# Streaming expert weights: a seventh weight buffer, and a token gather that reads the unscaled residual

## The reference

```python
h = rms_norm_2(x, norm_ffn_g[layer])          # x * rsqrt(mean(x*x) + eps) * gain
x = x + hier_moe(h, ...)                      # top-1 group of 4, then top-2 of its 8 experts

# hier_moe, for each chosen (token, expert):
#   y = gate * ((silu(h @ w_gate[e]) * (h @ w_up[e])) @ w_down[e])
```

## Time and profile before

| | |
|---|---|
| median of the runs | 1615.85 us |
| profiled execution, first to last instruction | 1614.8 us |
| TensorE busy | 1349.9 us (84%) |
| VectorE busy | 381.9 us (24%) |
| mean DMA rate over the span | 308 GB/s |
| DMA rate within the expert layers | 428 GB/s |

### The profile page before, as it was taken

How to read it: one execution, slowest core, us unless ns; L and a number is a source line. 1 busy time by engine, 2 the same in 40 slices (tenths; PEclk the granted TensorE clock), 3 DMA queues, 4 the chain that set the end, 5 groups by cost and what they waited for, 6 DMA issues and landing times. The chain is left out here.

```text
span 1614.8 us, 22089 instructions
## 1 busy us (share of the span) xinstructions
PE 1349.9 (84%) x9414; PEld 723.8 (45%) x9414; DVE 381.9 (24%) x787; ACT 278.1 (17%) x545; POOL 96.3 (6%) x98
## 2 busy tenths in 40 slices
PE   7999999999999999676676677899998667667676
PEld 3755457544879664232232232556553223232232
DVE  2331333313375531010010000257421001000011
ACT  1122310313223121210000000105211101111010
POOL 0000000000000006294000000000000000000000
PEclk9999999999999999989899898999999988899889
DMA  9822443234521199999999999934689999999997
GB/s 385 268 110 104 156 181 132 79 125 173 215 105 56 42 426 422 429 428 429 429 429 429 428 429 428 403 120 169 264 345 422 429 429 428 428 428 429 429 429 328
DMA packets 42092, 497.05 MB, mean 308 GB/s; under 512 B 6448, under 2 KB 9264, under 8 KB 11568
## 3 DMA queue, kind: packets, MB, share of 16 engines
q1 hardware_dynamic: 42032, 496.17, 74.5%
HBM read 494.06 MB, written 2.10 MB: 307 GB/s over the span
## 5 line engine op out<-in xcount | busy, mean ns | idle before, releaser
L2657 PE MATMUL banks<-weight_ring,arena 128*32 128x512 f32 x1920 | 286.2, 728 | 183.7 <-DMA weight_ring<-in_moe_weights 183.2
L2657 PEld LDWEIGHTS banks<-weight_ring,arena 128*32 128x32 f32 x1920 | 60.0, 121 | 389.2 <-DMA weight_ring<-in_moe_weights 201.0
L2580 DVE TENSOR_TENSOR arena<-arena,banks 64x512 f32<-64x512 f32 x32 | 22.1, 690 | 695.0 <-ACT arena L2528 694.0
L808 PE MATMUL banks<-weight_ring,hT 128*128 128x512 f32 x384 | 170.1, 600 | 1.3 <-DMA weight_ring<-in_ring_weights 1.3
L2668 PE MATMUL banks<-weight_ring,arena 128*32 128x512 f32 x1016 | 120.4, 602 | 27.6 <-issue 14.7
L2639 PE MATMUL banks<-arena,x_normed 128*128 128x64 f32 x1024 | 120.0, 276 | 0.0
L2639 PEld LDWEIGHTS banks<-arena,x_normed 128*128 128x128 f32 x1024 | 119.5, 195 | 0.0
L808 PEld LDWEIGHTS banks<-weight_ring,hT 128*128 128x128 f32 x384 | 73.0, 193 | 88.1 <-issue 86.3
L322 PE MATMUL banks<-weight_ring,hT 128*128 128x512 f32 x256 | 112.3, 593 | 0.0
L2528 ACT ACTIVATE arena<-banks 64x512 f32<-64x512 f32 x32 | 18.9, 591 | 522.1 <-PE banks L2657 522.1
L2698 PE MATMUL banks<-arena 64*128 64x512 f32 x240 | 59.6, 615 | 21.0 <-ACT arena L2534 21.0
(11 more groups left out here) (489 smaller groups left out, 1373.3 us busy)
## 6 DMA issues: line engine op xcount, KB each, us to landing
weight_ring<-in_moe_weights SPq DMA_DIRECT2D x183, 2048.0 KB, 26.2
weight_ring<-in_ring_weights SPq DMA_DIRECT2D x36, 2048.0 KB, 8.4
arena<-in_moe_weights SPq DMA_DIRECT2D x4, 2048.0 KB, 10.0
weight_ring<-in_ring_weights SPq DMA_DIRECT2D x4, 1024.0 KB, 4.8
mix<-in_moe_weights SPq DMA_DIRECT2D x2, 2048.0 KB, 16.4
arena<-in_moe_weights SPq DMA_DIRECT2D x3, 1024.0 KB, 13.1
hT<-in_moe_weights SPq DMA_DIRECT2D x2, 1024.0 KB, 9.9
arena<-in_c_even SPq DMA_DIRECT2D x1, 1440.0 KB, 6.4
```

What stands on the lines that cost most here:

```text
L808: ins = pe.matmul(bank, g.hT[:, k, half * P:(half + 1) * P], w[:, k, :], start=(k == 0), stop=(k == KT - 1))
L2580: dve.tensor_tensor(hid[0:2 * CAP, :], sil[0:2 * CAP, :], b_gu[2 * CAP:4 * CAP, :], ALU.mult).then_inc(s_h, 1)
L2657: ins = pe.matmul(b_gu[q:q + CAP, :], xg[:, 2 * quarter + k, e * CAP:(e + 1) * CAP], up_w(where, quarter, e)[:, which, k, :], start=(quart ...
```

## The change

- One more buffer of a full chunk, `g.spare`, holds (1,4). The room for it comes from the scratch that the compiler object reserves (`dynamic_dma_scratch_size=512`).
- `x_normed` is no longer filled by the router (`scale_x` is gone, and the squares go to a scratch that lies in `xg`), so a half of (1,5) goes there. The gather multiplies `g.x` itself, and the row factor 1/rms is multiplied into the selection matrix: `pick` now makes `Pm` (0/1) and, behind a wait, `Pr` = `Pm` times `rstd`.
- (1,5)'s other half goes into ring slot 0 in ly = 0, and into `xT_flat` in ly = 1.
- In ly = 0, (2,0) to (2,4) are issued when quarters 1, 2, 3 and the down halves of pair 0 are done, and (2,5) after pair 1's second down half. In ly = 1, (2,0) to (2,5) are issued after the six parts of pair 0.

```diff
+        self.spare = sb("spare_weights", [P, SW])[:, :]
+        self.xs_flat = self.xs[:, :, :].rearrange("p a d -> p (a d)")
...
@@ first expert layer, SyncE
             weights(1, 0, extra[0][0], second)
             weights(1, 1, extra[1][0], second)
+            weights(1, 4, g.spare, second)
+            sp.dma_start(g.xs_flat, A["moe_weights"][0, 1, 5][:, 0:2048]).then_inc(second[5], 16)
             router.fourth(sp)
...
@@ second expert layer, SyncE
+            weights(1, 4, g.spare, second)
             sp.wait_ge(s_prj, 5)
             weights(0, 0, ring[0], first)
...
             weights(1, 0, extra[0][0], second)
+            sp.dma_start(g.xs_flat, A["moe_weights"][1, 1, 5][:, 2048:SW]).then_inc(second[5], 16)
             sp.wait_ge(s_on, TT)
...
-            sp.dma_start(router.xT_flat, A["moe_weights"][1, 1, 4][:, 0:2048]).then_inc(second[4], 16)
+            sp.dma_start(router.xT_flat, A["moe_weights"][1, 1, 5][:, 0:2048]).then_inc(second[5], 16)
...
@@ VectorE
-        self.scale_x(dve, 1)
...
-        def pick(i):
-            dve.tensor_tensor(Pm, slots, of_pair(rankm, i), ALU.is_equal).then_inc(s_pm, 1)
+        def pick(i, n):
+            dve.tensor_tensor(Pm, slots, of_pair(rankm, i), ALU.is_equal).then_inc(s_eq, 1)
+            dve.wait_ge(s_eq, n + 1)
+            dve.tensor_tensor(Pr, Pm.rearrange("p a e j -> p a (e j)"),
+                              router.rstd.unsqueeze(2).to_broadcast([P, TT, 2 * CAP]), ALU.mult).then_inc(s_pm, 1)
...
@@ SyncE, expert phase
-        for j in range(4, 6):
-            released(j - 4, 0, 1)
-            load(1, 1, j)
+        if ly == 0:
+            released(0, 0, 1)
+            sp.dma_start(sixth[1], A["moe_weights"][ly, 1, 5][:, 2048:SW]).then_inc(landed[1][5], 16)
         for j in range(SLOTS):
-            released((2, 3, 4, 5, 4, 5)[j], 0, 1 if j < 4 else 2)
-            load(2, 2, j)
+            if j + turned < SLOTS:
+                released(j + turned, 0, 1)
+            else:
+                released(5, 0, 2)
+            load(2, j)
...
@@ TensorE, gather
-  g.xs[:, tt, k * P:(k + 1) * P], Pm[:, tt].rearrange("p e j -> p (e j)")
+  g.x[:, tt, k * P:(k + 1) * P], Pr[:, tt, :]
```

More of the change, by code:

```diff
@@ L45 @@
 MOE_AT = ODD_PAR
-MOE_SIZE = 3080
+MOE_SIZE = 3208
 SPLIT_AT = MOE_AT + MOE_SIZE
@@ L49 @@
 LAST_AT = EXTRA_AT + 2 * SW
-ARENA = 16960
-TURNED = 2
+ARENA = 17088
+TURNED = 1
 IN_ORDER = (4, 5, 0, 1, 2, 6, 3, 7)
@@ L336, with __init__ @@
 class TileNorm:
-    def __init__(self, g, sems, k, at, gain, banks):
+    def __init__(self, g, sems, bases, at, gain, banks):
         self.g, self.gain, self.banks = g, gain, banks
@@ L343, in __init__, with after @@
         self.s_sq, self.s_eps, self.s_rt, self.s_xs, self.s_tr, self.s_hT = \
-            (Counted(sem, k * n) for sem, n in zip(sems, (4, 2, 2, 2, 4, 4)))
+            (Counted(sem, base) for sem, base in zip(sems, bases))
+    def after(k):
+        return tuple(k * n for n in (4, 2, 2, 2, 4, 4))
     def sems(g, name):
@@ L472, in first_layers @@
     norm_sems = TileNorm.sems(g, "first_norm")
-    n_in = [TileNorm(g, norm_sems, 2 * l, (128, 144, 192)[l], gcol[l], (2, 3)) for l in range(DEPTH + 1)]
-    n_ple = [TileNorm(g, norm_sems, 2 * l + 1, 160 + 16 * l, None, (2, 3)) for l in range(DEPTH)]
+    n_in = [TileNorm(g, norm_sems, TileNorm.after(2 * l), (128, 144, 192)[l], gcol[l], (2, 3)) for l in range(DEPTH + 1)]
+    n_ple = [TileNorm(g, norm_sems, TileNorm.after(2 * l + 1), 160 + 16 * l, None, (2, 3)) for l in range(DEPTH)]
     layer = FirstSems.layers(g)
@@ L1369, in _ @@
                     router.inverse(dve, 0)
-                    router.scale_x(dve, 0)
                 if j == 2:
@@ L2245, in __init__ @@
         self.Pm = g.take(TT * 2 * CAP).rearrange("p (a e j) -> p a e j", a=TT, e=2)
+        self.Pr = g.take(TT * 2 * CAP).rearrange("p (a j) -> p a j", a=TT)
         self.w1 = self.Pm.rearrange("p a e j -> p a (e j)")[:, :, 0:NE]
@@ L2248, in __init__ @@
         self.PT = g.take(S)
-        self.xg = g.take(KT * 2 * CAP).rearrange("p (k j) -> p k j", k=KT)
+        xg = g.take(KT * 2 * CAP)
+        self.squared = xg[:, 0:HALF]
+        self.xg = xg.rearrange("p (k j) -> p k j", k=KT)
         self.hidT = g.take(4 * 2 * CAP).rearrange("p (f j) -> p f j", f=4)
@@ L2273, in squares @@
         act.wait_ge(self.s_x, j + 1)
-        act.activation(self.g.xs[:, tt, half], self.g.x[:, tt, half], ACT.Square,
+        act.activation(self.squared, self.g.x[:, tt, half], ACT.Square,
                        accum_out=self.part[:, j:j + 1]).then_inc(self.s_sq, 1)
@@ L2438, in expert_functions @@
     gcol, sil, hid, gate, rankm = router.gcol, router.sil, router.hid, router.gate, router.rankm
-    Pm, Pg, PT, xg, hidT, y = router.Pm, router.Pg, router.PT, router.xg, router.hidT, router.y
+    Pm, Pr, Pg, PT, xg, hidT, y = router.Pm, router.Pr, router.Pg, router.PT, router.xg, router.hidT, router.y
     s_pm, s_P, s_Pt, s_PTc = router.s_pm, router.s_P, router.s_Pt, router.s_PTc
@@ L2444, in expert_functions @@
     landed = g.moe_landed[ly]
-    fifth = [ring[0]] if ly == 0 else [router.xT_flat, ring[0][:, 0:2048]]
-    at_pair = ([[w] for w in ring], extra + [fifth, [ring[1]]], [[ring[(j + 2) % SLOTS]] for j in range(SLOTS)])
+    sixth = [g.xs_flat, ring[0][:, 0:2048]] if ly == 0 else [router.xT_flat, g.xs_flat]
+    turned = 1 - ly
+    at_pair = ([[w] for w in ring], extra + [[g.spare], sixth], [[ring[(j + turned) % SLOTS]] for j in range(SLOTS)])
     def up_w(where, j, e):
@@ L2462, in expert_functions @@
     s_da, s_dn, s_yc = (g.sem(n_ + k) for k in ("down_half", "down", "y_copied"))
-    s_sub, s_add = g.sem(n_ + "ranks_lowered"), g.sem(n_ + "added")
+    s_sub, s_add, s_eq = g.sem(n_ + "ranks_lowered"), g.sem(n_ + "added"), g.sem(n_ + "P_compared")
     s_sum = [g.sem(n_ + f"summed_{b}") for b in range(4)]
@@ L2482, in released, with load @@
             sp.wait_ge(*((s_gu, n * 4 + (more * 4 + j - 3)) if j < 4 else ((s_da, s_dn)[j - 4], n + more)))
[L2485 to L2491, removed]
-        for j in range(4, 6):
-            released(j - 4, 0, 1)
-            load(1, 1, j)
-        for j in range(SLOTS):
-            released((2, 3, 4, 5, 4, 5)[j], 0, 1 if j < 4 else 2)
-            load(2, 2, j)
+        def load(pair, j):
+            sp.dma_start(at_pair[2][j][0], A["moe_weights"][ly, pair, j]).then_inc(landed[2][j], 16)
+        if ly == 0:
+            released(0, 0, 1)
+            sp.dma_start(sixth[1], A["moe_weights"][ly, 1, 5][:, 2048:SW]).then_inc(landed[1][5], 16)
+        for j in range(SLOTS):
+            if j + turned < SLOTS:
[3 more added lines that the diff above has]
+            load(2, j)
         if ly == 0:
@@ L2506, in sync @@
                     released(j, t * NP + i, 3)
-                    load(2, i + 3, j)
+                    load(i + 3, j)
             with sp.If(t < T - 1):
@@ L2511, in sync @@
                         released(j, t * NP, pair + NP)
-                        load(2, pair, j)
+                        load(pair, j)
         g.limit = len(g.chunks)
@@ L2587, in advance @@
             gated(of_next, n + 1)
-        pick(0)
+        pick(0, 0)
         router.largest(dve)
@@ L2594, in vector @@
         gated(0, 0)
-        pick(1)
+        pick(1, 1)
         router.count_turns(dve)
@@ L2604, in vector @@
                 advance(t * NP + i, i + 1)
-                pick(i + 2)
+                pick(i + 2, t * NP + (i + 2))
             advance(t * NP + (NP - 2), NP - 1)
@@ L2608, in vector @@
             dve.wait_ge(s_sub, t + 1)
-            pick(0)
+            pick(0, t * NP + NP)
             advance(t * NP + (NP - 1), 0)
-            pick(1)
+            pick(1, t * NP + (NP + 1))
         def added(j):
@@ L2638, in gather @@
                 for tt in range(TT):
-                    ins = pe.matmul((b_x, b_dn)[k // 4][:, k % 4 * 2 * CAP:(k % 4 + 1) * 2 * CAP], g.xs[:, tt, k * P:(k + 1) * P],
-                                    Pm[:, tt].rearrange("p e j -> p (e j)"), start=(tt == 0), stop=(tt == TT - 1))
+                    ins = pe.matmul((b_x, b_dn)[k // 4][:, k % 4 * 2 * CAP:(k % 4 + 1) * 2 * CAP], g.x[:, tt, k * P:(k + 1) * P],
+                                    Pr[:, tt, :], start=(tt == 0), stop=(tt == TT - 1))
                 if k % 4 == 3:
@@ L2846 @@
     from concourse.bass_utils import run_bass_kernel_spmd as _run
-    nc = _bacc.Bacc("TRN2", target_bir_lowering=False, num_devices=1)
+    nc = _bacc.Bacc("TRN2", target_bir_lowering=False, num_devices=1, dynamic_dma_scratch_size=512)
     arrays = laid_out(inputs)
```

4 lines of the change are left out of this document (1 added, 3 removed).

## The result

The changed kernel takes 1623.09 us (median of 5 runs, 1621.04 to 1623.9), the kernel before 1616.77 us beside it (5 runs, 1615.61 to 1619.04). The ratio is 1.0039, with a 95% interval of 1.0028 to 1.005: slower by about 6.3 us, outside the range of the prediction and on the other side of "no change". The profiled execution has a span of 1621.3 us, 6.5 more than before.

The account below looks back on a forecast made before the run. The prediction took full DMA engines in both expert layers to bound the kernel. A 4.2 us loss in the first less a 3.4 us gain in the second gave +0.8 on 1615.85, so 1616.6 us, range 1612.3 to 1619.6.

Parts of the forecast that it names:

- The sum was +0.8 us: Whole kernel: first expert layer 4.2 us late, less 3.4 us gained in the second; -0.8 without the clock's fall.
- Second expert layer, gain 3.4 us: Second expert layer: (3,0) flows from 1217.6 instead of 1221.0 us, because pair 0 releases all of pair 2.
- First expert layer, the wait for `odd_par`: First expert layer: 1.5 chunks go ahead of odd_par, which lands 7.3 us later; TensorE's down starts 6.0 us late.
- The clock, 1.6 us: First expert layer: one fall to half clock after TensorE's wait, 1.6 us more until pair 1 releases (2,5).
- The DMA gap: First expert layer, ahead of (2,5): queue idle 3.1 us, plus 1.6 us for the clock's fall.
- The added early transfers of this layer are free: Second expert layer: the spare's transfer and x_normed's half move while the queue is empty or largely idle, costing nothing.
- The selection and the gather, 0 to 0.1 us: Both expert layers: pick's second operation adds 0 to 0.1 us on the path; the gather stays at 3.68 us.
- Rival 2: First expert layer: lateness grows, half clock over down 0 and pair 1's gate and up; 1620.3 us, chance 0.08.
- Rival 3: Second expert layer: a clock fall in pair 1 or 2 cuts its gain to 1.8; 1618.3 us, chance 0.10.
- Rival 1: First expert layer: odd_par overtakes the chunks ahead, TensorE never stalls, no cost there; 1612.4 us, chance 0.13.

Follow-up runs that it names:

- e5_gather_only: Changed kernel's selection, gather and missing scaling, with the queue, buffers and release schedule of the kernel before: 1615.75 us, ratio 0.9998 to the kernel before.
- e9_half_transfer: Kernel before plus an unread 1024 KB transfer into the spare buffer at the start of the odd mixer: 1616.23 us, ratio 1.0001 to the kernel before.
- e3_both: Changed kernel with first-layer spare and x_normed transfers behind odd_par, and second-layer spare transfer behind (1,0): 1612.03 us, ratio 0.9973 to the kernel before.
- e10_late_in_second: e3_both with the second expert layer's spare and x_normed transfers issued last ahead of the expert phase: 1611.98 us, ratio 0.9974 to the kernel before.
- e1_params_first: Changed kernel with the first expert layer's spare chunk and x_normed half issued behind odd_par: 1617.83 us, ratio 1.0005 to the kernel before.
- e4_before_plus_transfer: Kernel before plus an unread 2048 KB transfer into the spare buffer at the start of the odd mixer: 1621.17 us, ratio 1.0037 to the kernel before.
- e2_spare_later: Changed kernel with the second layer's spare transfer moved from the start of the odd mixer to behind (1,0): 1618.06 us, ratio 1.0011 to the kernel before.

## Why the prediction was wrong

**The sum was +0.8 us, and 6.3 were measured.** Step by step:

- *Second expert layer, gain 3.4 us: right.* With before's release schedule and no fall of the clock in pair 0, the layer takes 425.54 us (e5_gather_only) and 425.56 (e9_half_transfer); with the new one 422.12 (e3_both), 422.20 (e10_late_in_second). That is 3.4 us. The profiled execution of before, at 427.33, had a fall in pair 0's down (5.26 us for 3.64) that these do not have, so the difference of 4.75 in the table is partly that. That the gain is capped by (3,0), and does not come from the number of early bytes, e10 shows.
- *First expert layer, the wait for `odd_par`: right in mechanism and place.* VectorE went on at 603.59 in a layer that began 0.84 us earlier; 604.1 was forecast (596.7 + 7.3 is 604.0). TensorE stood for 6.07 us; 6.0 was forecast. e1_params_first took the wait away and with it the loss.
- *The clock, 1.6 us: too small.* I took the row where 16 matmuls ran at half clock. Here the clock fell within the wait and stayed down to 612, so the transposes lost 0.38 and the 32 matmuls of down 2.32: **2.7 us**. The DMA gap was 5.2 us and not 3.1 + 1.6, and the layer came out 4.82 us late instead of 4.2.
- *"The added early transfers of this layer are free": wrong. This is the step that failed.* I read the row of 1060 to 1070 (2 GB/s) as room for the transfer and put its cost at nothing. I did not ask who else needs those engines. The 256 small matmuls ran beside nearly empty DMA engines before; beside full ones the packet with their instructions came 2.5 us later and they ran out: 2.47 us for the group and 2.34 for the 48 long matmuls behind it, the first of which ran at half clock. The stretch is 5.29 us longer; its last 0.5 us is the fall in the router, below. e4_before_plus_transfer shows the loss (4.8 us in the median, 3.3 in the odd mixer of its profiled execution) with nothing else of the change but the buffer and the smaller scratch, which e9_half_transfer has too without the loss; e2_spare_later takes it out of the changed kernel (5.0 us).
- *The selection and the gather, 0 to 0.1 us: right*, by e5_gather_only (0.12 us on the path, no difference in time).
- *The router, not forecast: +1.98 us in the profiled execution.* TensorE's 40 clock-keeping matmuls (products of constants that nothing reads, issued while the router works) took 7.49 us instead of 4.71, at a granted clock of 0.50 from 1174 to 1178. e1_params_first has it (15.08 us), e2_spare_later a part of it (13.87), and e3_both (13.19) and e10_late_in_second (13.19) do not have it. Where it is, the transfer at the start of the odd mixer or the wait in the first layer is there too; but e4 has the transfer and no fall in the router (13.07). Why it comes is open.

Rival 2 named the side on which it would end, but its reason, a longer fall of the clock in the first layer, brought 1.1 us of the loss and not the stall. Its 1.8 + 3.5 us also do not follow from the rows: at 1.6 us for 16 matmuls, half clock over all of down and of gate and up would be 3.2 + 6.4. Rival 3, nothing gained in the second layer, is refuted. Rival 1, that the parameters overtake, fell with the 603.59.

## What to carry to other kernels

Idle DMA engines are not free for the taking where an engine runs through many short instructions: look at the density of instructions beside a new bulk transfer (35 matmuls in each us stalled here, 16 to 20 did not), and put it beside long ones. Before moving bytes to the front of an in-order queue, list what they are moved past, and who waits for each; a small parameter transfer can hold an engine that holds the one that frees the buffers. A prefetch is worth what the next release lets through, not the bytes it moves: find the first transfer behind the gap, and what frees its place.

## What the runs showed of the hardware

The instructions of an engine come over the same DMA engines as the data, and bulk data delays them. The page of the profile has a queue of kind "instruction" (47 packets, 0.77 MB over the whole kernel). The trace does not name the engine that a packet is for; that these are TensorE's follows from the 166th matmul, which starts 1.28 to 1.37 us after the packet's end in all four kernels where it is late. With 2048 KB in the way the wait is 1.08 to 1.20 us long; with 1024 KB the 166th matmul is 0.3 us late. How a DMA engine orders the packets of two queues is not shown.

The Trainium skill (Runtime: NRT & Kernel Launch, "Instruction fetch mechanics") says that the sequencer fetches its next instructions through a DMA queue of its own while it executes the current ones, and that the cost is mostly hidden. The trace agrees with the queue. The cost is hidden here with idle engines, and with full ones beside 16 to 20 matmuls in each us; it is not with full ones beside 35, each with its weight load.

After each of the three stalls the granted clock fell to 0.50 within 3 us; none of the eight other traces has a fall in this stretch. In e1_params_first the fall came at once, the 91 small matmuls behind the stall took 5.38 us instead of 3.25 in e4_before_plus_transfer, and the stretch 156.52 us; in e4 it took 152.87. So the same stall of 1.20 us cost 6.9 us in one execution (0.5 of it the fall in the router) and 3.3 in another.
